# ScalarE rounds 35 up projection chunks a layer that GpSimd rounded before

## The reference, cut to what matters

```
u = rmsnorm(x, g_pre_ffn) @ w_up                  # (T,1024) @ (1024, 2*2816)
uc = conv_b;  uc += u_ext[:, i:i+T] * conv_w[i]   # causal, width 3, over positions
gate, val = uc[..., :2816], uc[..., 2816:]
f = (gelu(gate) * val) @ w_down                   # (T,2816) @ (2816,1024)
x = x + rmsnorm(f, g_post_ffn)
x = x + sigmoid(x @ w_ple_gate) * (p @ w_ple_proj)
```

## Time and the profile before

| | |
|---|---|
| median of 3 runs | 1817.53 us (1816.24 to 1818.27) |
| the profiled execution: span, first to last instruction | 1815.9 us |
| the profiled execution's own time | not given apart; its span lies 1.6 us under the median and 0.3 us under the fastest run |
| PE busy | 1800.5 us, 99% of the span |
| DVE, ACT, POOL busy | 1133.6, 664.3, 1189.2 us (62%, 37%, 65%) |
| granted clock of TensorE | 1.000 over the whole span |

### The profile page before, as it was taken

How to read it: one execution, slowest core, us unless ns; L and a number is a source line. 1 busy time by engine, 2 the same in 40 slices (tenths; PEclk the granted TensorE clock), 3 DMA queues, 4 the chain that set the end, 5 groups by cost and what they waited for, 6 DMA issues and landing times.

```text
span 1815.9 us, 34638 instructions
## 1 busy us (share of the span) xinstructions
PE 1800.5 (99%) x14006; PEld 1742.0 (96%) x14006; DVE 1133.6 (62%) x1952; ACT 664.3 (37%) x1433; POOL 1189.2 (65%) x1396
## 2 busy tenths in 40 slices
PE   9999999999999999999999999999999999999999
PEld 8998889999999999999999988899999999999999
DVE  6676775332779579554656767752337895795554
ACT  4444553112535235323334444531134352352221
POOL 8685634656675875967676864346467759759584
PEclk9999999999999999999999999999999999999999
DMA  5242211324222222323342421122332223223232
GB/s 185 96 125 80 72 42 59 106 87 153 78 82 94 93 91 86 100 69 101 106 142 92 138 76 59 61 69 84 134 101 82 82 94 94 93 86 101 73 94 96
DMA packets 76239, 170.54 MB, mean 94 GB/s; under 512 B 6384, under 2 KB 34160, under 8 KB 76080
## 3 DMA queue, kind: packets, MB, share of 16 engines
q1 hardware_dynamic: 68752, 160.79, 27.7%
q10 hardware_dynamic: 7328, 7.54, 1.3%
HBM read 156.41 MB, written 9.79 MB: 92 GB/s over the span
## 4 chain that ended last, share of the span: by engine, by line
PE 88%; DVE 9%; ACT 2%; issue 1%; DMA 0%; POOL 0%; SPq 0%; DVEq 0%; ACTq 0%; POOLq 0%
PE ps L1958 59%; PE ps L2396 7%; PE ps L2011 4%; PE ps L2426 4%; PE ps L2139 3%; PE ps L2097 2%; DVE R L1342 1%; DVE xT L1701 1%; PE ps L2193 1%; PE ps L2050 1%; DVE mix L1697 1%; PE ps L2199 1%; DVE xn L1342 1%; PE ps L1998 1%; PE ps L2116 1%
## 5 line engine op out<-in xcount | busy, mean ns | idle before, releaser
L1958 PE MATMUL ps<-xn,wsp 128*128 128x272 f32 x7728 | 989.8, 289 | 3.1 <-DVE xn L1317 1.4
L1958 PEld LDWEIGHTS ps<-xn,wsp 128*128 128x128 f32 x7728 | 974.1, 189 | 7.7 <-issue 2.7
L760 POOL TENSOR_TENSOR wsp<-raw,wsp 128x256 fp32r<-128x256 f32 x656 | 514.3, 805 | 26.2
L755 POOL CAST wsp<-raw 128x512 fp32r<-128x512 f32 x328 | 223.4, 681 | 255.1 <-DMA raw<-in_wstream 198.0
L773 POOL TENSOR_TENSOR wsp<-raw,wsp 128x256 fp32r<-128x256 f32 (+1 forms) x174 | 212.5, 1243 | 6.6
L1958 PE MATMUL ps<-R,wsp 128*128 128x272 f32 x1632 | 209.4, 289 | 0.2 <-ACT RF L838 0.2
L766 POOL CAST wsp<-raw 128x1024 fp32r<-128x1024 f32 (+2 forms) x102 | 91.5, 907 | 178.4 <-DMA raw<-in_wstream 159.6
L1958 PEld LDWEIGHTS ps<-R,wsp 128*128 128x128 f32 x1632 | 206.0, 189 | 1.7 <-DVE xT L1371 0.5
L1342 DVE SCALAR_TENSOR_TENSOR R<-ps,R 128x512 fp32r<-128x512 f32 (+13 forms) x272 | 129.4, 499 | 65.7 <-ACT R L855 20.0
L748 POOL TENSOR_TENSOR wsp<-raw,wsp 128x512 fp32r<-128x512 f32 x64 | 94.4, 1496 | 68.0 <-DVE raw L1795 34.1
L1729 DVE SCALAR_TENSOR_TENSOR ps<-mix,vv,ps 128x546 f32<-128x546 f32 x88 | 69.5, 790 | 63.6 <-ACT ps L1177 63.6
(11 more groups left out here) (280 smaller groups left out, 2304.9 us busy)
## 6 DMA issues: line engine op xcount, KB each, us to landing
raw<-in_wstream SPq DMA_DIRECT2D x233, 512.0 KB, 3.6
raw<-in_wstream SPq DMA_DIRECT2D x48, 128.0 KB, 2.6
raw<-in_wstream SPq DMA_DIRECT2D x16, 384.0 KB, 3.2
raw<-in_kc SPq DMA_DIRECT2D x8, 512.0 KB, 3.5
raw<-in_vc SPq DMA_DIRECT2D x8, 512.0 KB, 4.3
xT<-in_x_in SPq DMA_DIRECT2D x8, 272.0 KB, 5.9
out_k_out<-mix ACTq DMA_DIRECT2D x8, 272.0 KB, 3.0
xT<-in_x_in SPq DMA_DIRECT2D x1, 2176.0 KB, 9.1
```

What stands on the lines that cost most here:

```text
L755: nc.gpsimd.tensor_copy(dst[:, 0, f], part[:, f]).then_inc(S["w_hi"], 1)
L760: ins = nc.gpsimd.tensor_tensor(dst[:, 1, f], part[:, f], dst[:, 0, f].bitcast(F32), ALU.subtract)
L1958: mm = pe.matmul(z[:, h], w[:, x, (k0 + k) * P:(k0 + k + 1) * P], rhs[:, y, k, h * HT:(h + 1) * HT], start=(k == 0 and (x, y) == (0, 0)), ...
```

## The change

The list `CAST` holds the up chunks whose third predecessor in the stream is an up chunk too: 15, 13 and 7 in the three runs, 35 a layer, 70 in all. For these ACT writes the whole high part in one instruction of 128x1024, at the end of the `u_tile` of the chunk three places before. GpSimd makes only the low parts, in four pieces of 256 columns, after it has waited for ACT's copy; `w_half` now comes after the second piece and `w_lo` after the fourth. PE's waits are unchanged. The first three up chunks of each run stay as they were. The rest of the diff gives several semaphores one name for both layers, with counts raised to match.

```
+UP = ("upg", "upv")
+CAST = [c for n, c in enumerate(STREAM) if c[0] in UP and STREAM[n - 3][0] in UP]
...
+        SPLIT_AFTER = {last_tile(STREAM[ST_AT[c] - 3]): c for c in CAST}
...
+                        if ch in CAST:
+                            pool.wait_ge(pre["cast"], len(CAST) * layer + CAST.index(ch) + 1)
+                            for j in range(4):
+                                f = slice(j * w // 4, (j + 1) * w // 4)
+                                ins = nc.gpsimd.tensor_tensor(dst[:, 1, f], part[:, f], dst[:, 0, f].bitcast(F32), ALU.subtract)
+                                if j % 2:
+                                    ins.then_inc(S["w_lo" if j == 3 else "w_half"], 1)
+                            continue
                         if ch in HALVED:
...
+                    def cast(c):
+
+                        slot = ring_slot(layer, c)
+                        act.wait_ge(raw_in[slot], 16 * LOADS[layer * NST + ST_AT[c]])
+                        ac(wsp[:, slot, 0], raw[:, slot, 1], ACT.Copy).then_inc(pre["cast"], 1)
...
                         ac(uc[v], e[:, 0:T + 2], ACT.Identity, scale=vv[:, V_CW + f:V_CW + f + 1],
                            bias=vv[:, V_CB + f:V_CB + f + 1]).then_inc(S["conv0"], 1)
+                        if t in SPLIT_AFTER:
+                            cast(SPLIT_AFTER[t])
```

More of the change, by code:

```diff
@@ L595, in build @@
                  "ones_set cache_used "
-                 "x_st x_back c_hi c_lo c_st rope_done rope_hi rope_lo kr_st "
+                 "c_hi c_lo c_st rope_done rope_hi rope_lo kr_st "
                  "m_neg e_done p_scaled sig "
                  "mi_raw mi_hi mi_lo conv0 tail_done conv2 gelu_done g_raw g_hi g_lo "
-                 "p_in p_hi p_lo conv_st").split()
+                 "p_hi p_lo").split()
         with ExitStack() as st:
             pre = {n: st.enter_context(nc.semaphore(n)) for n in
-                   ("con_in", "late_in", *(f"x_in{k}" for k in range(KT)), "c_in", "y_done0", "y_gate0", "y_raw0", "qr_in", "made", "eps_made", "squares", "added", "summed", "logs", "roots", "sum_raw", "sum_hi",
+                   ("con_in", "late_in", *(f"x_in{k}" for k in range(KT)), "c_in", "y_done0", "y_gate0", "y_raw0", "qr_in", "made", "cast", "x_st", "x_back", "p_in", "conv_st", "squares", "added", "summed", "logs", "roots", "sum_raw", "sum_hi",
                     "y_st")}
@@ L679, in _ @@
                     if layer > 0:
-                        sp_.wait_ge(S["x_st"], 16)
-                    sp_.dma_start(xT[:], x_dram if layer > 0 else x_in.rearrange("(k p) t -> p k t", p=P)).then_inc(S["x_back"], 16)
-                    sp_.dma_start(mix[:, 0:2, 0:T], p_in[layer].rearrange("(k p) t -> p k t", p=P)).then_inc(S["p_in"], 16)
+                        sp_.wait_ge(pre["x_st"], 16)
+                    sp_.dma_start(xT[:], x_dram if layer > 0 else x_in.rearrange("(k p) t -> p k t", p=P)).then_inc(pre["x_back"], 16)
+                    sp_.dma_start(mix[:, 0:2, 0:T], p_in[layer].rearrange("(k p) t -> p k t", p=P)).then_inc(pre["p_in"], 16)
                     load_to(ST_AT[("down", LAST, 2)])
                     sp_.wait_ge(S["tail_done"], 2 * FT)
-                    sp_.dma_start(conv_out[layer], ctail[:]).then_inc(S["conv_st"], 16)
+                    sp_.dma_start(conv_out[layer], ctail[:]).then_inc(pre["conv_st"], 16)
                     if layer < DEPTH - 1:
@@ L692, in _ @@
                     load_to(NST)
-                    sp_.wait_ge(S["conv_st"], 16)
+                    sp_.wait_ge(pre["conv_st"], 16 * (layer + 1))
                     if layer == DEPTH - 1:
@@ L787, in _ @@
                     nc.scalar.activation(start_sq[k], xT[:, k], ACT.Square).then_inc(pre["squares"], 1)
-                act.wait_ge(pre["eps_made"], 1)
+                act.wait_ge(pre["made"], 1)
                 act.wait_ge(pre["summed"], 1)
@@ L1061, in _ @@
                     if layer > 0:
-                        act.dma_start(x_dram, xT[:]).then_inc(S["x_st"], 16)
+                        act.dma_start(x_dram, xT[:]).then_inc(pre["x_st"], 16)
                     c_tile()
@@ L1074, in _ @@
                     if layer > 0:
-                        act.wait_ge(S["x_st"], 16)
+                        act.wait_ge(pre["x_st"], 16)
                     else:
@@ L1139, in _ @@
                         if j in (4, 5):
-                            act.wait_ge(S["p_in"], 16)
+                            act.wait_ge(pre["p_in"], 16 * (layer + 1))
                             ac(p_s[:, 0, j - 4], mix[:, j - 4, 0:T], ACT.Copy).then_inc(S["p_hi"], 1)
@@ L1312, in _ @@
                 nc.vector.memset(rstd[:], 0.0)
-                nc.vector.memset(epsb[:], EPS).then_inc(pre["eps_made"], 1)
+                nc.vector.memset(epsb[:], EPS).then_inc(pre["made"], 1)
                 dve.wait_ge(SS[0]["vec_in"], 16)
@@ L1599, in _ @@
                     if layer > 0:
-                        dve.wait_ge(S["x_st"], 16)
+                        dve.wait_ge(pre["x_st"], 16)
                     v_tile(("v", 0))
@@ L1691, in residual @@
                         dve.wait_ge(S["rstd_done"], which)
-                        dve.wait_ge(S["x_back"], 16)
+                        dve.wait_ge(pre["x_back"], 16 * (layer + 1))
                         dve.wait_ge(S["act_read" if last[0] == "out" else "dve_read"], (aread if last[0] == "out" else dread)(last))
@@ L1912, in _ @@
             def _(pe):
-                pe.wait_ge(pre["eps_made"], 1)
+                pe.wait_ge(pre["made"], 1)
                 for k in range(KT):
@@ L2278, in _ @@
                     if layer == 0:
-                        pe.wait_ge(pre["made"], 2)
+                        pe.wait_ge(pre["made"], 3)
                     for s in range(STEPS):
```

## The result

The changed kernel takes 1829.26 us (median of 4 runs, 1827.45 to 1831.56), the kernel before 1817.47 us (4 runs). The ratio is 1.0064, 95% interval 1.0050 to 1.0078: slower by 11.8 us, where 7.2 were forecast. The profiled execution took 1827.97 us; its span is 1826.2 us, 10.3 more than before.

A forecast was written before the change was run, and what follows sets the result against it. The prediction took PE at its own matmul pace as the bound; waits of 3.1 + 3.3 + 0.4 + 0.4 = 7.2 us added to 1817.5 gave 1824.7 us, range 1822.3 to 1828.3 us.

The forecast's parts named there:

- What bounds the kernel: Up runs: PE at its pace, 124.7 ns a matmul, waits for nothing; GpSimd work removed there was already hidden.
- the rival that GpSimd's traffic slows TensorE: Up runs: less GpSimd traffic makes PE faster; 0.9 ns a matmul brings time within 0.2% of before; chance 0.04.
- The two waits for upv 1: Start of each layer's up part: upv 1's copy queues behind ACT's first tap; PE waits 3.1 and 3.3 us.
- The wait for upv 2: Two chunks after upv 1 starts: upv 2's high part comes late; PE waits 0.4 us in both layers.
- The steady pairs: Later up chunks: copies cost nothing, with 4.8 us in hand for weights and 0.1 us cover before the product.
- The sum: Whole kernel: waits of 3.1 + 3.3 + 0.4 + 0.4 = 7.2 us, giving 1824.7 us.
- The first rival: At the upv 1 waits: TensorE's clock falls, some 1.5 us each, 3 us on top, 1828 us; chance 0.1.
- Relief on DVE: DVE's split instructions freer of POOL shorten PE's remaining waits, at most 2 us back, 1822.7 us; chance 0.06.
- The paid-back wait: After the up-part waits: later waits vanish and about half returns, 1821 us, within 0.2%; chance 0.04.

The follow-up runs named there:

- filled kernel: The changed kernel plus 24 extra matmuls of 272 columns on PE before it waits for upv 1, their result overwritten: 1824.21 us, ratio 1.0036 to the kernel before.
- the last version: The changed kernel with upv 1's copy before the norm's Ln, upg 2's behind Exp, upv 2's behind the first pair's gelu: 1816.84 us, ratio 0.9993.
- the longer wait: The changed kernel with the copies of upv 1 and upg 2 both behind the tap of upv 0 on ACT: 1836.78 us, ratio 1.0103.

## What the prediction had right, and the step that failed

**What bounds the kernel** held. In the middle of the first run of up chunks PE does the same number of matmuls as in the earlier trace rows, 481 in 60 us, with GpSimd at 50% instead of 74% (windows: length, PE, PEld, DVE, ACT, POOL, clock):

```profile
506.00:566.00 60.00, 60.00 (x481) 60.00 (x481) 45.83 (x92) 32.50 (x72) 30.17 (x41) 1.00 0.27 88
```

This also disposes of the rival that GpSimd's traffic slows TensorE: no nanosecond was given back. By the Trainium skill, "SBUF — State Buffer", section "Who interferes with whom", TensorE waits for nobody; the trace agrees, with 481 matmuls in 60 us before and after.

**The two waits for upv 1**, forecast at 3.1 and 3.3 us, measured 3.33 us each: from the last start before to the first after are 3.455 and 3.454 us, less the usual 0.125. Copy (1.04) and first pieces (1.40) were as forecast; the hand-overs were larger, 0.17 us from ScalarE to GpSimd and 0.15 to PE, against 0.08 in all. **The wait for upv 2**, forecast 0.4, measured 0.5 in each layer (0.622 and 0.606 us between two starts, less 0.125). These four are 7.7 us. In the filled kernel's trace they are 7.5 (3.26 and 0.49 in each layer), and it lost 6.6 us: the difference is about the size of the relief below, and within the interval of its ratio (4.2 to 8.7 us).

**The steady pairs** cost nothing, as said. The version without upv 1 shows it in the time (1.0002).

**The step that failed is the clock.** The sum put the clock's fall at nothing, and the prediction expected a granted clock of 1.00 through the waits; the runs showed falls in both layers that cost 5.1 us. The first rival had this mechanism, but it got a chance of 0.1, on the argument that in the last 3.5 us of the trace, with PE idle, the clock still stood at 1.00. That was one execution. All ten profiled executions end with 3.5 to 3.6 us without a matmul, and in three of them the clock falls there; in the last version after 2.3 us, for the rest of the trace (a window of PE as above):

```profile
1813.60:1814.80 1.20, 0.00 (x0) 0.53 0.25 89
```

Beside the pauses above, where the fall came between 2.1 us (the longer wait, layer 1) and 4.3 us after the last matmul, a window of 3.5 us that stays at 1.00 says little: the fall can be just behind it, as in layer 0, where it came when PE was already at work again. The other ground, "TensorE: Matmul & The Clock Gate" in the Trainium skill, section "HAM oscillation", by which a long enough pause puts the next burst at the low level, should have weighed more with a wait as long as the one forecast. The trace agrees with it in layer 1, where PE starts at 0.50; in layer 0 the burst's first 1.1 us still ran at 1.00.

**The rival's price was right by luck where it fitted, and short in all.** It gave 1.5 us for each fall, and in the profiled run 13.77 - 12.30 and 13.67 - 12.30 give 1.5 and 1.4. But it was read from the slow first matmuls of the trace, and in their window, 1.40 to 6.00 us, the granted clock reads 1.00, so those rows don't show a low clock. Over the runs the clock's part, from the filled kernel to the changed one, is 1829.26 - 1824.21 = 5.1 us, not 3. The executions of the changed kernel show two kinds: 1827.97 and 1827.45 us at a mean clock of 0.998, 1831.56 and 1830.54 at 0.996. At half speed, 0.998 means some 7 us at the low level in all and 0.996 some 15, so in the second kind there were further or longer low stretches (7 us more of them would cost about 3.6 us, and the kinds lie 2.6 to 4.1 us apart), and the median lies between the two. Where they lie stays open, since only one execution was profiled, one of the first kind.

**Relief on DVE** exists and is small, as forecast. DVE's two-input instructions that split the saved parts, by form, before and now:

```profile
L1342 DVE SCALAR_TENSOR_TENSOR R<-RF,R 128x272 fp32r<-128x272 f32 x64 | 47.6, 744 | 0.1
L1364 DVE SCALAR_TENSOR_TENSOR R<-RF,R 128x272 fp32r<-128x272 f32 x64 | 34.5, 540 | 0.1
```

Not all forms gained: R<-mix of 128x272 went from 775 to 814 ns. DVE as a whole is busy 18.9 us less. PE's wait on GpSimd at the down projection (L2396 in the earlier trace rows, L2418 now) fell only from 1.1 to 0.8 us. With all stalls moved away, the last version puts the worth of the whole relief at about 0.9 us, which its interval doesn't tell from nothing.

**The paid-back wait** did not occur. Between two versions whose clock stayed up, the one with the copy between Exp and tap and the filled one, the waits for upv 1 and upv 2 grow by 4.0 us in the traces and the time over the kernel before by 4.6: what is waited there comes out at the end.

So of the 11.8 us: about 6.6 are the waits net of the small relief, 5.1 the clock.

## What to carry to other kernels

A step moved to an engine with idle time is not free until you have looked, at each boundary between stages, at what stands in front of it in that engine's order; here 34 of 35 copies cost nothing that the times could tell, and one, queued behind the result of a norm, cost nearly everything. In a kernel whose TensorE never pauses, price the first pause of about 3 us twice: once for itself and once for the clock, and look for the fall both in the pause and in the first microseconds behind it. One trace whose clock stays up through such a pause doesn't show that the next will. Here the cure was not to undo the move but to place the first copies by hand where the engine waited anyway.

## What the runs showed of the hardware

- The granted clock fell to 0.5 at all four pauses of TensorE of 3.17 and 3.44 us (profiled runs of the changed kernel and of the one with upv 1 alone) and at both of 6.67 us. At 2.74 and 2.75 us it stayed at 1.00 in the profiled run; the mean clocks of the four other runs (0.998 and 0.999) suggest that it fell in some of them. At 1.12 us it stayed up, and the mean clock was 1.000 in 11 of 11 runs.
- The fall can come inside the pause or behind it, in one and the same kernel: in the changed kernel 1.1 us into the following work in layer 0 and 0.3 us before the end of the pause in layer 1.
- A low stretch was 3.4 us long behind or at the pauses of 3.17 and 3.44 us, and 10.2 us at those of 6.67 us.
- 24 matmuls whose result is thrown away (3.17 us) kept the clock at 1.00 through the same wait and made the kernel 5.1 us faster. A wait shorter by 0.43 us a layer took off nearly as much (5.0 us).
